# Five norms sum their squares over tiles on VectorE before the matmul with ones

## The chip, the cores and the metric

The kernel runs on one core of a Trainium2 chip, in one launch. The metric is the device time of an execution in microseconds (us), the median over several runs. The engines named here are TensorE (PE in the profile, PEld for its weight loads), VectorE (DVE), ScalarE (ACT), GpSimd (POOL) and SyncE (SP), which issues the transfers.

## The reference, cut to what matters

Two blocks are computed for 256 tokens of width 1024: a block with latent attention, a Fourier mixer and a hierarchical mixture of 32 experts, and then a two-layer block with a context of 256 tokens, attention, a convolution and several gated FFNs (width 2816). Between the parts stands the same norm, with a modulation by shift and scale:

```python
def rmsnorm_2(x, g):
    x32 = x.astype(jnp.float32)
    y = x32 * lax.rsqrt(jnp.mean(x32 * x32, axis=-1, keepdims=True) + EPS)
    return (y * g.astype(jnp.float32)).astype(x.dtype)

def modulate_2(x, g, shift, scale):
    return rmsnorm_2(x, g) * (1 + scale) + shift

def swiglu(x, w_gate, w_up, w_down):
    return (jax.nn.silu(x @ w_gate) * (x @ w_up)) @ w_down

def macaron_ffn(xs, g, shift, scale, gate, w_gate, w_up, w_down):
    return xs + 0.5 * gate * swiglu(modulate_2(xs, g, shift, scale), w_gate, w_up, w_down)
```

There are twelve norms in the kernel, numbered 0 to 11. The change is about norms 2 to 6: 2 is the context's ahead of its FFN, 3 the one that ends the first block, 4 the latent's ahead of its first FFN, 5 and 6 those of context and latent ahead of the attention.

## The kernel before

The state is held transposed: HT (latent) and CT (context) are SBUF tiles of 128 partitions by 8 tiles by 256 tokens, so that the 1024 features lie over partitions and tiles. Each engine has its program in a fixed, handwritten order, and works through it in that order; semaphores tie the engines together.

**Weights.** They come as pages of 128x2048 in float32 from device memory. SyncE issues a page into one of three slots of `raw`; ScalarE copies it rounded into `W` (`split`, L1494, or L1616 for the experts) and GpSimd subtracts that from the page for the remainder (`rest`, L632; L685 and, for the last expert unit in halves, L690 in the trace). TensorE takes each product three times: high by high, low by high, high by low (`mm3`, L703 to L705). A slot comes free when GpSimd has read it, and a place in W when TensorE has used it.

**A norm**, in the order of its steps:
- ScalarE squares the state into `XR`, two of the eight tiles at a time (`norm_squares`, L1466), each of the four steps with an increment of the semaphore `norm_squares` (`s_sq`).
- TensorE multiplies each of the eight tiles of XR with a 128x128 tile of ones and lets them add up in PSUM (`norm_chunk`, L737). This gives each partition the sum over all 1024 features. Float32 operands make two records of each of these matmuls in the trace, 16 for a norm.
- ScalarE takes the root (`norm_root`, L1476), for which it loads another activation table.
- VectorE makes the gains NA_ from scale and weight (`norm_head`, L1868), the reciprocal of the root (`norm_coef`, L1847), and scales the eight tiles (`norm_tiles`, L1879).
- ScalarE adds the shift with rounding (`norm_scaled`, L1485), VectorE makes the remainder (`norm_low`, L1858). Norm 3 has no remainder; its result is the state HT itself, and behind it ScalarE makes the squares of norm 4 at once.

**An FFN pass** (`ff_pass`: ctx_ff, ff00, ff01, ff10, ff11) has 11 units of three pages. In a unit TensorE makes the gate and up products of two halves (j = 0, 1) in PSUM banks, ScalarE the Silu of each (L1513) and behind it the split of the page three places on, VectorE multiplies, rounds and subtracts (L1925 to L1927, the last one makes HL), and TensorE makes the down products. Between them TensorE takes a column product of the modulation (`mod_product`, L728) whose vector VectorE summed in the unit before (`mod_sum`, L1826 and L1828) and takes from PSUM in this one (`mod_take`, L1837).

**Where the five norms stand.** Norms 3 and 4 stand in the pass ctx_ff, behind its units 0 and 2, and norm 5 in ff00, behind unit 1: on TensorE as `mid_norm`, which first waits for the unit's modulation and then makes the eight matmuls, on VectorE behind the unit's `mod_sum`, and on ScalarE behind the unit's last split and ahead of the next unit's Silu. Norm 2 stands among the last expert units: squares on ScalarE in unit 35, the matmuls on TensorE behind unit 37's first steps and the down products of unit 36, the root in unit 37. Norm 6 stands behind ff00: TensorE makes one product of the attention's projection (kac0), the norm, and another one (kac1).

Of the kernel before, what the change touches and what calls it, by code (L numbers as in the profile page):

```python
# [23 lines left out]
S = 256  # L24
# [72 lines left out]
NUNIT = GSLOTS * NE8  # L97
# [5 lines left out]
def build(nc, pages, mpages, acts, vecs, mbias, small):  # L103
# [4 lines left out]
    with ctx:  # L108
# [5 lines left out]
        def sem(name):  # L114
            if name not in sems:
                sems[name] = ctx.enter_context(nc.semaphore(name))
            return sems[name]
# [151 lines left out]
        def bias_of(h):  # L269
# [26 lines left out]
                                                  sem("group_aux"), sem("group_aux_copied"))  # L296
        s_silu = sem("silu_done")
        s_sq = sem("norm_squares")
        s_rt, s_ri, s_xr, s_yf, s_y = (sem("norm_root"), sem("norm_coef"), sem("norm_scaled"), sem("norm_result"),
                                         sem("norm_split"))  # L300
        s_xs = sem("norm_plain")
# [157 lines left out]
        def opened(pe, name, i=0):  # L459

            if prev_free[name, i] is not None:
                pe.wait_ge(*prev_free[name, i])
            return bank(name, i)
# [24 lines left out]
        NCH = 4  # L488
# [3 lines left out]

        SPLITS = [sum(1 for x in NORMS[:n] if x[1] in OPERANDS) for n in range(len(NORMS) + 1)]
        N_SMALL, N_MID = 10, 4
        MID_NORM = {"ctx_ff": ((1, "ss3"), (3, "ss4")), "ff00": ((2, "ss5"),), "ff01": (), "ff10": (), "ff11": ()}


# [200 lines left out]
        def _(pe):  # L698
# [40 lines left out]
                    last.then_inc(s_tile, 1)  # L739

            def norm(n):
                for c in range(NCH):
                    norm_chunk(n, c)

# [1047 lines left out]
        def _(dve):  # L1792
# [47 lines left out]
            def mod_step(m, vectors=(1,), i=0):  # L1840

                mod_sum(m, vectors, i)
                mod_take(m - 1, i, len(vectors))

            def norm_coef(n):
                dve.wait_ge(*tiles[f"ss{n}", 0][2])
                v.reciprocal(RT[:, 0:S], RT[:, 0:S]).then_inc(s_ri, 1)  # L1847
                dve.wait_ge(s_ri, n + 1)
# [40 lines left out]
            def residual(name, coef):  # L1889

                dst, col = coef
                for q in range(4):
                    ps = filled(dve, name, q)
                    for b in range(2):
                        k = 2 * q + b
                        last = v.scalar_tensor_tensor(out=dst[:, k, :], in0=ps[:, b * S:(b + 1) * S], scalar=col(k),
                                                      in1=dst[:, k, :], op0=ALU.mult, op1=ALU.add)
                    free(last, name, q)
# [4 lines left out]
            def half_gate(c, vi=0):  # L1903
                link(v.tensor_scalar(HG[:], MODT[:, c:c + KD, vi], 0.5, None, ALU.mult))
                return lambda k: HG[:, k:k + 1]

            def ff_pass(name, between=()):
                p0, u0, n, src, acc, parts = PASSES[name]
                steps = 2
                hx0 = hx[0]  # L1910

                def unit(u, i, vectors):
                    U = u0 + u
                    for j in range(2):
                        done = [hx0 + steps * (2 * u + j)]

                        def step(ins):

                            done[0] += 1
                            ins.then_inc(s_hx, 1)  # L1920
                            dve.wait_ge(s_hx, i * 4 * steps + done[0])

                        dve.wait_ge(s_silu, i * 4 + (2 * U + j + 1))
                        sil, hid = SIL[:, j, :], PS[GU[j]][:, S:2 * S]
                        step(v.tensor_tensor(hid, hid, sil, ALU.mult))  # L1925
                        step(v.tensor_copy(HH[:, j, :], hid))
                        v.tensor_tensor(HL[:, j, :], hid, HH[:, j, :].bitcast(f32), ALU.subtract).then_inc(s_hid, 1)  # L1927
                    if vectors:
                        mod_take(MOD_AT[name] + u - 1, i, len(vectors[1]))
                        if MOD_AT[name] + u < NMODP and not (u == n - 1 and name in TAIL):  # L1930
                            mod_sum(MOD_AT[name] + u, vectors[0], i)

                units(dve, parts, unit, between)
                hx[0] += steps * 2 * n
# [328 lines left out]
            def expert_low(u, part):  # L2263
                dve.wait_ge(s_mhi, 2 * u + part + 1)
                v.tensor_tensor(PAIRL[u % 2][:, part].rearrange("p k n -> p (k n)"), expert_raw(u, part),
                                PAIRH[u % 2][:, part, :].bitcast(f32), ALU.subtract).then_inc(low_done(u, part)[0], 1)
# [7 lines left out]
            for u in range(NUNIT):  # L2274
                j, e = u // NE8, u % NE8
                dve.wait_ge(s_gsil, u + 1)
                if u:
                    dve.wait_ge(s_gturn, u)
                if e == 0:
                    dve.wait_ge(s_auxd, 2 * (j + 1))  # L2280
                v.scalar_tensor_tensor(out=HID, in0=SIL[:, u % 2, :].rearrange("p (j n) -> p j n", j=2), scalar=CWS[:, j, e:e + 1],
                                       in1=PS[2 + u % 2][:, :].rearrange("p (j g n) -> p j g n", j=2, g=2)[:, :, 1, :],
                                       op0=ALU.mult, op1=ALU.mult).then_inc(s_ghid, 1)
                if u == 0:
                    mod_sum(20, (0,))
                if u in MOD_UNITS:
                    k = MOD_UNITS.index(u)
                    vectors = (0,) if k < MOE_ADA else (1, 2)
                    mod_sum(MOD_AT["moe"] + k, vectors)
                    mod_take(MOD_AT["moe"] + k - 1, 0, len(vectors))  # L2290
                if j and e == 0:
                    out_low(j - 1)
                if j and 1 <= e <= 4:
                    if e == 1 and j == 1:
                        dve.wait_ge(s_modev, (ADA + 48) // 2)
                    add_tokens(j - 1, e - 1)
                if j + 1 < GSLOTS:
                    if e == 4:
                        onehot(j + 1)
                    elif e in (5, 6):  # L2300
                        gathered_lo(j + 1, e - 5)
                    elif e == 7:
                        aux_copy(j + 1)
                if (u + 2, 1) in BY_VECTOR:
                    expert_low(u + 2, 1)
                if u == NUNIT - 3:
                    norm_head(2)
                if u == NUNIT - 2:
                    norm_tiles(2, range(0, 5), low=False)
                if u == NUNIT - 1:  # L2310
                    norm_tiles(2, range(5, KD), low=False)
                    for q in range(KD):
                        norm_low(2, q)
# [5 lines left out]
            residual("acc_ctx", (CT, half_gate(MOD0 + 16, 1)))  # L2319
            ff_pass("ff00", (lambda: None, lambda: norm(5)))  # L2320
            residual("acc_00", (HT, half_gate(MOD0 + 16, 0)))
            mod_take(MOD_AT["mixer"] - 1)
            norm(6)
            dve.wait_ge(sem("in_mid"), 16 * N_MID)
# [300 lines left out]
```

## Time and profile before

| | |
|---|---|
| median of 3 runs | 2045.34 us (2042.76 to 2045.85) |
| the profiled execution | 2042.77 us, of which the span from first to last instruction is 2041.0 |
| mean granted TensorE clock | 0.989 of full speed |
| TensorE busy | 1968.1 us (96%) |
| TensorE weight loads | 1768.6 us (87%) |
| VectorE busy | 1020.0 us (50%) |
| ScalarE busy | 824.4 us (40%) |
| GpSimd busy | 1329.9 us (65%) |

The span is what the profiler saw of one execution; 1.8 us of its time lie outside. Matmul records overlap, so a busy time near the span says that the engine's queue was hardly ever empty, not that each matmul ran at its best. An idle stretch of an engine carries the name of what released it. The norms in question lie at 662 (norm 2), 711 (norm 3), 750 (norm 4), 932 (norm 5) and 1100 us (norm 6) of the span.

### The profile page before, as it was taken

The page shows a single profiled execution, that of the slowest core. Times are in us where ns is not written, and L with a number is a line of the kernel's source. Part 1 is how long each engine was busy: PE and PEld are TensorE (multiplying, and loading weights), DVE is VectorE, ACT ScalarE, POOL GpSimd, SP SyncE. Part 2 cuts the span into 40 slices and gives each one's busy share as a digit, 9 for nine tenths or more (in the row PEclk, how much of TensorE's full clock was granted, in tenths as well). Part 3 has the DMA queues.
Part 4 walks back from the last instruction along what each step waited for, and adds up shares of the span by engine and source line. Part 5 has one row for each costly group of instructions (what it writes and reads, how often), then busy time and mean ns, then how long its engine had stood idle before and what let it go on. Part 6 is the DMA issues. An engine that isn't in the chain of part 4 may idle for free.

```text
span 2041.0 us, 34520 instructions
## 1 busy us (share of the span) xinstructions
PE 1968.1 (96%) x13902; PEld 1768.6 (87%) x13902; DVE 1020.0 (50%) x2154; ACT 824.4 (40%) x874; POOL 1329.9 (65%) x310
## 2 busy tenths in 40 slices
PE   6999889999999999999999999899999999999998
PEld 4879767667676799999999769799999999999998
DVE  6767474558565465455336334453335334654212
ACT  4343354444444553334434332443344333434332
POOL 5727157776768668777775412377777777777884
PEclk8999899999999999999999999999999999999999
DMA  8537198989898655666665402156665666655552
GB/s 354 214 124 289 67 374 349 376 345 368 355 375 336 230 224 210 244 239 225 241 241 205 153 33 104 60 215 242 247 239 204 233 233 244 229 221 192 185 185 83
DMA packets 67414, 473.92 MB, mean 232 GB/s; under 512 B 8064, under 2 KB 9184, under 8 KB 10208
## 3 DMA queue, kind: packets, MB, share of 16 engines
q1 hardware_dynamic: 65344, 466.82, 60.2%
q10 hardware_dynamic: 1952, 5.44, 0.7%
q8 instruction: 85, 1.39, 0.3%
q14 instruction: 33, 0.27, 0.0%
HBM read 471.18 MB, written 1.05 MB: 231 GB/s over the span
## 4 chain that ended last, share of the span: by engine, by line
PE 48%; issue 23%; POOL 19%; DMA 6%; DVE 1%; ACT 1%; SPq 0%; POOLq 0%; ACTq 0%; DVEq 0%
POOL W L632 15%; PE bank L703 11%; PE bank L705 11%; PE bank L704 11%; DMA raw<-in_pages 6%; PE bank L1197 4%; POOL YC L685 2%; PE bank L709 2%; PE bank L711 2%; PE bank L710 2%; PE bank L737 1%; ACT W L1616 1%; PE bank L728 1%; PE bank L748 1%; POOL W L685 1%
## 5 line engine op out<-in xcount | busy, mean ns | idle before, releaser
L632 POOL TENSOR_TENSOR W<-raw,W 128x2048 fp32r<-128x2048 f32 x220 | 1014.0, 4614 | 518.9 <-ACT W L1494 518.8
L703 PE MATMUL bank<-YH,W 128*128 128x256 f32 x1936 | 551.2, 285 | 1.1 <-POOL W L632 0.8
L705 PE MATMUL bank<-YH,W 128*128 128x256 f32 x1936 | 547.7, 283 | 0.0
L704 PE MATMUL bank<-YL,W 128*128 128x256 f32 x1936 | 547.6, 283 | 0.0
L1494 ACT ACTIVATE W<-raw 128x2048 fp32r<-128x2048 f32 x220 | 420.1, 1909 | 302.0 <-PE bank L705 275.6
L703 PEld LDWEIGHTS bank<-YH,W 128*128 128x128 f32 x1936 | 371.0, 192 | 3.9 <-POOL W L632 1.2
L704 PEld LDWEIGHTS bank<-YL,W 128*128 128x128 f32 x1936 | 371.3, 192 | 0.4 <-issue 0.2
L705 PEld LDWEIGHTS bank<-YH,W 128*128 128x128 f32 x1936 | 371.2, 192 | 0.0
L1828 DVE SCALAR_TENSOR_TENSOR bank<-mraw,CA,bank 128x256 f32<-128x256 f32 x696 | 329.1, 489 | 20.3
L1925 DVE TENSOR_TENSOR bank<-bank,SIL 128x256 f32<-128x256 f32 x110 | 47.6, 433 | 540.9 <-ACT SIL L1513 540.9
L703 PE MATMUL bank<-HH,W 128*128 128x256 f32 x880 | 249.7, 284 | 0.5 <-DVE HL L1927 0.4
L705 PE MATMUL bank<-HH,W 128*128 128x256 f32 x880 | 245.6, 279 | 0.0
L704 PE MATMUL bank<-HL,W 128*128 128x256 f32 x880 | 245.4, 279 | 0.0
L1616 ACT ACTIVATE W<-raw 128x2048 fp32r<-128x2048 f32 x77 | 147.5, 1916 | 147.5 <-DMA raw<-in_pages 147.5
L685 POOL TENSOR_TENSOR W<-raw,W 128x2048 fp32r<-128x2048 f32 x30 | 137.2, 4590 | 89.8 <-ACT W L1616 89.8
L685 POOL TENSOR_TENSOR YC<-raw,W 128x2048 fp32r<-128x2048 f32 x33 | 150.6, 4585 | 67.9 <-ACT W L1616 67.9
L1513 ACT ACTIVATE SIL<-bank 128x256 f32<-128x256 f32 x110 | 42.2, 384 | 359.1 <-PE bank L705 357.6
L703 PEld LDWEIGHTS bank<-HH,W 128*128 128x128 f32 x880 | 165.7, 188 | 0.7 <-issue 0.4
L704 PEld LDWEIGHTS bank<-HL,W 128*128 128x128 f32 x880 | 165.6, 188 | 0.0
L705 PEld LDWEIGHTS bank<-HH,W 128*128 128x128 f32 x880 | 165.4, 188 | 0.0
L709 PE MATMUL bank<-W,YH 128*128 128x512 f32 (+1 forms) x392 | 150.3, 383 | 9.0 <-POOL YC L685 6.6
L703 PE MATMUL bank<-YC,W 128*128 128x256 f32 (+1 forms) x536 | 153.5, 286 | 1.0 <-DVE R L2015 1.0
(353 smaller groups left out, 3159.5 us busy)
## 6 DMA issues: line engine op xcount, KB each, us to landing
raw<-in_pages SPq DMA_DIRECT2D x299, 1024.0 KB, 4.9
mraw<-in_mpages SPq DMA_DIRECT2D x98, 1024.0 KB, 6.9
R<-in_pages SPq DMA_DIRECT2D x24, 1024.0 KB, 5.8
XR<-in_pages SPq DMA_DIRECT2D x17, 1024.0 KB, 5.5
R<-in_mpages SPq DMA_DIRECT2D x4, 1024.0 KB, 16.3
HT<-in_acts ACTq DMA_DIRECT2D x1, 1024.0 KB, 14.1
CT<-in_mpages SPq DMA_DIRECT2D x1, 1024.0 KB, 19.4
raw<-in_mpages SPq DMA_DIRECT2D x1, 1024.0 KB, 25.1
```

What stands on the lines that cost most here:

```text
L632: nc.gpsimd.tensor_tensor(WL[:, p % SLOTS, :], raw[:, p % SLOTS, :], WH[:, p % SLOTS, :].bitcast(f32), ALU.subtract).then_inc(s_lo, 1)
L685: p_.tensor_tensor(PAIRL[u % 2][:, part].rearrange("p k n -> p (k n)"), expert_raw(u, part), PAIRH[u % 2][:, part, :].bitcast(f32), ALU.su ...
L703: mm(out, w[0], x[0], start=start, stop=False, skip_group_check=True)
L704: mm(out, w[0], x[1], start=False, stop=False, skip_group_check=True)
L705: return mm(out, w[1], x[0], start=False, stop=stop, skip_group_check=True)
L709: mm(out, x[0], w[0], start=start, stop=False, skip_group_check=True)
L1197: last = mm(PS[OUT[n]][:, :], HTT[:, j, :], w[:, j * D + n * 512:j * D + n * 512 + 512], start=(u % NE8 == 0 and j == 0), stop=(u % NE8 == ...
L1494: f(WH[:, p % SLOTS, :], raw[:, p % SLOTS, :], ACT.Copy).then_inc(s_hi, 1)
L1513: f(SIL[:, j, :], PS[GU[j]][:, 0:S], ACT.Silu).then_inc(s_silu, 1)
L1616: f(PAIRH[u % 2][:, part, :], expert_raw(u, part), ACT.Copy).then_inc(s_mhi, 1)
L1828: last = v.scalar_tensor_tensor(out=out, in0=w[:, k, :], scalar=c, in1=part, op0=ALU.mult, op1=ALU.add)
L1925: step(v.tensor_tensor(hid, hid, sil, ALU.mult))
```

## The change

For norms 2 to 6 VectorE adds the eight tiles of squares to one, in place, in three linked steps: tiles 4 to 7 to tiles 0 to 3 (128x1024), then 2 and 3 to 0 and 1 (128x512), then 1 to 0 (128x256). A new semaphore tells TensorE, which then makes one matmul with ones in place of eight. `link` makes VectorE wait for the end of the instruction before it goes on. The steps stand behind the products HL and ahead of `mod_take` in unit 0 of ctx_ff (norm 3), unit 2 of ctx_ff (norm 4) and unit 0 of ff00 (norm 5); at the end of expert unit 36 (norm 2, NUNIT is 40); and straight behind the residual of ff00 (norm 6).

```diff
+        PRESUMMED = (2, 3, 4, 5, 6)
+        PRESUM_AT = {("ctx_ff", 0): 3, ("ctx_ff", 2): 4, ("ff00", 0): 5}
...
             def norm(n):
+                if n in PRESUMMED:
+                    ps = opened(pe, f"ss{n}")
+                    pe.wait_ge(s_presum, PRESUMMED.index(n) + 1)
+                    mm(ps[:, 0:S], ONES[:], XR[:, 0, :], start=True, stop=True, skip_group_check=True).then_inc(s_tile, 1)
+                    return
                 for c in range(NCH):
                     norm_chunk(n, c)
...
+            def presum(n):
+                dve.wait_ge(s_sq, NCH * (n + 1))
+                link(v.tensor_tensor(XR[:, 0:4, :], XR[:, 0:4, :], XR[:, 4:8, :], ALU.add))
+                link(v.tensor_tensor(XR[:, 0:2, :], XR[:, 0:2, :], XR[:, 2:4, :], ALU.add))
+                v.tensor_tensor(XR[:, 0, :], XR[:, 0, :], XR[:, 1, :], ALU.add).then_inc(s_presum, 1)
...
                         v.tensor_tensor(HL[:, j, :], hid, HH[:, j, :].bitcast(f32), ALU.subtract).then_inc(s_hid, 1)
+                    if (name, u) in PRESUM_AT:
+                        presum(PRESUM_AT[name, u])
                     if vectors:
                         mod_take(MOD_AT[name] + u - 1, i, len(vectors[1]))
...
                 if (u + 2, 1) in BY_VECTOR:
                     expert_low(u + 2, 1)
+                if u == NUNIT - 4:
+                    presum(2)
                 if u == NUNIT - 3:
                     norm_head(2)
...
             residual("acc_00", (HT, half_gate(MOD0 + 16, 0)))
+            presum(6)
             mod_take(MOD_AT["mixer"] - 1)
             norm(6)
```

The order of VectorE's instructions around norm 3, before the change (unit 0 of ctx_ff; HL is the second remainder of the unit, MODT the modulation taken, MACC its next sum, NA_ the gains, RT the root):

```order
L1927 TENSOR_TENSOR HL<-bank,HH 128x256
L1837 TENSOR_TENSOR MODT<-bank,MB 128x4
L1826 TENSOR_SCALAR bank<-mraw,CA 128x256
L1828 SCALAR_TENSOR_TENSOR bank<-mraw,CA,bank 128x256 x6
L1828 SCALAR_TENSOR_TENSOR MACC<-mraw,CA,bank 128x256
L1868 SCALAR_TENSOR_TENSOR NA_<-MODT,V 128x8
L1847 RECIPROCAL RT<-RT 128x256
```

and with the change (its line numbers are higher, as lines were added):

```order
L1941 TENSOR_TENSOR HL<-bank,HH 128x256
L1855 TENSOR_TENSOR XR<-XR 128x1024
L1856 TENSOR_TENSOR XR<-XR 128x512
L1857 TENSOR_TENSOR XR<-XR 128x256
L1845 TENSOR_TENSOR MODT<-bank,MB 128x4
L1834 TENSOR_SCALAR bank<-mraw,CA 128x256
L1836 SCALAR_TENSOR_TENSOR bank<-mraw,CA,bank 128x256 x6
L1836 SCALAR_TENSOR_TENSOR MACC<-mraw,CA,bank 128x256
L1882 SCALAR_TENSOR_TENSOR NA_<-MODT,V 128x8
L1861 RECIPROCAL RT<-RT 128x256
```

The three adds stand ahead of everything that leads to the reciprocal. The order of TensorE's instructions at the same place before, from the last down product of unit 0 (HH, HL) to the first gate product of unit 1 (YC):

```order
L704 MATMUL bank<-HL,W 128x256
L705 MATMUL bank<-HH,W 128x256
L737 MATMUL bank<-XR,ONES 128x256 x8
L703 MATMUL bank<-YC,W 128x256
L704 MATMUL bank<-YC,W 128x256
```

and with the change:

```order
L707 MATMUL bank<-HL,W 128x256
L708 MATMUL bank<-HH,W 128x256
L748 MATMUL bank<-XR,ONES 128x256
L706 MATMUL bank<-YC,W 128x256
L707 MATMUL bank<-YC,W 128x256
```

Eight matmuls became one, and nothing else moved. VectorE's instructions at norm 6 with the change, behind the residual of ff00 (before, the three adds are missing and the rest is the same):

```order
L1910 SCALAR_TENSOR_TENSOR HT<-bank,HG,HT 128x256 x8
L1855 TENSOR_TENSOR XR<-XR 128x1024
L1856 TENSOR_TENSOR XR<-XR 128x512
L1857 TENSOR_TENSOR XR<-XR 128x256
L1845 TENSOR_TENSOR MODT<-bank,MB 128x2
L1882 SCALAR_TENSOR_TENSOR NA_<-MODT,V 128x8
L1861 RECIPROCAL RT<-RT 128x256
```

Here too the take of the modulation, the gains and the reciprocal stand behind the adds.

## Rows read from the trace of the kernel before

**Rows 1.** TensorE timeline, norm 2: start, duration (us), engine, line, operation, tiles.

```profile
662.28 3.62 PE L737 MATMUL bank<-XR,ONES 128*128 128x256 f32 x16
...
665.54 0.58 PE L709 MATMUL bank<-W,YH 128*128 128x512 f32 x1
```

**Rows 2.** TensorE timeline, norm 3; in brackets: idle time ahead, its releaser.

```profile
710.72 3.62 PE L737 MATMUL bank<-XR,ONES 128*128 128x256 f32 x16
...
726.55 0.36 PE L703 MATMUL bank<-HH,W 128*128 128x256 f32 x1 [0.37 <-DVE HL L1927]
```

**Rows 3.** Timeline of ScalarE (ACT) at norm 3.

```profile
714.37 0.47 ACT L1476 ACTIVATE RT<-bank,EPSC 128x256 f32<-128x256 f32 x1 [0.24 <-PE bank L737]
...
724.64 0.38 ACT L1513 ACTIVATE SIL<-bank 128x256 f32<-128x256 f32 x1
```

**Rows 4.** Timeline of VectorE (DVE) at norm 3.

```profile
705.76 0.42 DVE L1927 TENSOR_TENSOR HL<-bank,HH 128x256 fp32r<-128x256 f32 x1
...
710.23 2.23 DVE L1868 SCALAR_TENSOR_TENSOR NA_<-MODT,V 128x8 f32<-128x8 f32 x1
714.95 1.75 DVE L1847 RECIPROCAL RT<-RT 128x256 f32<-128x256 f32 x1 [2.49 <-ACT RT L1476]
```

**Rows 5.** Source view (ns min/median/max), GpSimd's (POOL) timeline, VectorE's groups by form.

```profile
L2058 DVE TENSOR_TENSOR XR<-XR,ST x6: 691/692/2573, 108.5 to 129.7; 128x512 f32<-128x512 f32 x6
...
105.99 4.51 POOL L632 TENSOR_TENSOR W<-raw,W 128x2048 fp32r<-128x2048 f32 x1 [1.61 <-ACT W L1494]
...
L1887 DVE TENSOR_TENSOR YL<-XR,YH 128x1024 fp32r<-128x1024 f32 x1 | 1.2, 1224 | 0.0
```

**Rows 6.** Timeline of VectorE and of GpSimd in expert work.

```profile
301.02 4.50 DVE L2192 TENSOR_SCALAR R<-CT,R 128x128 f32<-128x128 f32 x1
305.44 4.61 DVE L2192 TENSOR_SCALAR R<-CT,R 128x128 f32<-128x128 f32 x1
305.39 4.57 POOL L685 TENSOR_TENSOR W<-raw,W 128x2048 fp32r<-128x2048 f32 x1
```

**Rows 7.** Window view (busy by engine, then granted clock); TensorE's timeline there.

```profile
300.00:310.00 10.00, 7.64 (x21) 4.59 (x20) 9.96 (x4) 3.83 (x2) 10.00 (x4) 0.83 0.86 340
...
305.53 0.47 PE L709 MATMUL bank<-W,YH 128*128 128x512 f32 x1 [2.36 <-POOL YC L685]
```

**Rows 8.** Timeline of GpSimd at norm 3.

```profile
703.28 9.15 POOL L632 TENSOR_TENSOR W<-raw,W 128x2048 fp32r<-128x2048 f32 x2 [3.58 <-ACT W L1494]
...
712.90 4.58 POOL L632 TENSOR_TENSOR W<-raw,W 128x2048 fp32r<-128x2048 f32 x1 [0.47 <-ACT W L1494]
```

**Rows 9.** Timeline of GpSimd at norm 2.

```profile
652.87 9.15 POOL L685 TENSOR_TENSOR W<-raw,W 128x2048 fp32r<-128x2048 f32 x2
661.96 2.37 POOL L690 TENSOR_TENSOR YH<-raw,W 128x1024 fp32r<-128x1024 f32 x1
```

**Rows 10.** Timeline of VectorE and of GpSimd at norm 4.

```profile
745.29 0.42 DVE L1927 TENSOR_TENSOR HL<-bank,HH 128x256 fp32r<-128x256 f32 x1
754.48 1.75 DVE L1847 RECIPROCAL RT<-RT 128x256 f32<-128x256 f32 x1 [3.58 <-ACT RT L1476]
746.28 4.59 POOL L632 TENSOR_TENSOR W<-raw,W 128x2048 fp32r<-128x2048 f32 x1 [1.02 <-ACT W L1494]
```

**Rows 11.** Timeline of VectorE, GpSimd and TensorE at norm 5.

```profile
909.75 0.42 DVE L1927 TENSOR_TENSOR HL<-bank,HH 128x256 fp32r<-128x256 f32 x1
916.45 4.62 POOL L632 TENSOR_TENSOR W<-raw,W 128x2048 fp32r<-128x2048 f32 x1 [1.17 <-ACT W L1494]
926.14 0.36 PE L703 MATMUL bank<-HH,W 128*128 128x256 f32 x1
```

**Rows 12.** Timeline of GpSimd and TensorE at norm 6.

```profile
1095.74 4.63 POOL L632 TENSOR_TENSOR W<-raw,W 128x2048 fp32r<-128x2048 f32 x1 [1.17 <-ACT W L1494]
1099.95 3.61 PE L737 MATMUL bank<-XR,ONES 128*128 128x256 f32 x16
...
1111.65 0.39 PE L703 MATMUL bank<-YH,W 128*128 128x256 f32 x1 [0.17 <-DVE YL L1858]
```

More of the change, by code:

```diff
@@ L298, in build @@
         s_sq = sem("norm_squares")
+        s_presum = sem("squares_summed_over_tiles")
         s_rt, s_ri, s_xr, s_yf, s_y = (sem("norm_root"), sem("norm_coef"), sem("norm_scaled"), sem("norm_result"),
```

## The prediction

> **What bounds the kernel now.** I read the page's totals first, then each engine's timeline around the five norms, because a share of busy time doesn't say which wait ends last at one place. TensorE is the busiest engine, and a norm with eight matmuls holds it for a clear stretch: norm 2's first record starts at 662.28 us and the next work at 665.54, so 3.26 us [rows 1]. One of the eight is an eighth of that, about 0.41 us. If TensorE's queue alone sets the pace, the removal is therefore worth 3.26 - 0.41 = 2.85 us of TensorE at each norm, 14.3 us for five.
>
> At norm 3 it doesn't. The norm's matmuls run at 710.72, and TensorE then has a unit's gate and up products to do, which don't need the norm. But at 726.55 it stood idle for 0.37 us, waiting for HL of VectorE [rows 2]. That HL hangs on another chain, which begins with the norm: ScalarE takes the root at 714.37 (0.24 us behind the last norm matmul; its activation table had only just been loaded), VectorE takes the reciprocal at 714.95, eight tiles are scaled and the next norm's squares made, and only then does ScalarE, in its program order, get to the unit's Silu at 724.64 [rows 3, 4]. So behind a norm inside an FFN pass two chains of nearly the same length meet. Shortening TensorE's alone turns the gain into a wait; what counts is when VectorE can take the reciprocal. The reader should keep that in mind: any delay of VectorE before 714.95 moves 726.55 one for one.
>
> **What the adds cost VectorE.** Alone, an add of 128x1024 should take the 1.22 us of a VectorE subtraction of that shape, and one of 128x512 the 0.69 us of the median in the same group [rows 5]; for 128x256 I take 0.42 us, the time of the subtraction HL [rows 4]. Sum 2.33 us, some 2.4 with the waits between. But the adds read two SBUF tiles, and the trace shows what such a VectorE instruction does while GpSimd works. The six multiplications of 128x512 take 0.691 us, except the first, 2.573: it was issued at 108.5 while GpSimd was in a subtraction from 105.99 to 110.50, and it ended about 0.6 us after that one [rows 5]. Two small ones that came one behind the other took 4.50 and 4.61 us [rows 6]. The first had been waiting since 301.02 and was done at 305.52, though GpSimd had issued its next page at 305.39; the second was issued at 305.44, 0.05 us behind that page, and waited until the page's end at 309.96. So: such an instruction waits until the running GpSimd instruction ends, whoever was issued first goes first, and between two of them a waiting GpSimd instruction gets in. Three linked adds then pay the rest of one GpSimd instruction and up to two whole ones of 4.57 us.
>
> The Trainium skill (SBUF — State Buffer, Who interferes with whom) speaks against this change in the same way: a VectorE instruction with two SBUF inputs contends with a GpSimd instruction that reads SBUF, and the pair of ports is held for the whole instruction. By this rule the three adds would take 6 to 13 us where GpSimd's queue is full, and 2.4 us without it. The trace agrees, with 2.573 us against 0.691.
>
> **TensorE's clock.** A wait of TensorE of 2.36 us at 305.53 lies in a stretch of 10 us with a mean granted clock of 0.83: 1.7 us of work lost, as a part of it ran at 1.2 instead of 2.4 GHz [rows 7]. I charge 1.7 us once for each new wait over 2 us, less what slack there is behind it.
>
> **Norm 3 (first unit of ctx_ff).** Everything of the adds stands before the take of the modulation, its sum, the gains NA_ and the reciprocal. The last HL ends at 706.18 [rows 4]. GpSimd has two pages from 703.28 to 712.43, the second from about 707.85, and a third is ready at 712.90 [rows 8]. First add: waits until 707.85, ends 709.07. GpSimd's second page moves to 709.07-713.64. Second add ends 714.33, third page ends 718.9, third add ends 719.3. TensorE can't start its norm matmul at 710.72 but at about 719.5. On VectorE the take and the sum need 4.1 us (706.1 to 710.23) [rows 4]; they now end at 723.5, NA_ at 723.7, as GpSimd is then idle. The reciprocal moves from 714.95 to 723.8, by 8.85 us. Before, the first scaled tile also waited about 0.55 us for the third page (ending 717.48); this wait is gone. So Silu and the unit's down products move by **+8.3 us**. TensorE's own work (0.4 + 11.7 us from 719.5, with the slow clock 1.7 more) ends near 733.3 and is hidden by that.
>
> **Norm 2 (expert unit 36).** The adds are issued while GpSimd is in the first of two pages (652.87 to 662.02, the second from about 657.45); then come four half pages of 2.4 us, the first at 661.96 [rows 9]. First add 657.45-658.67, page to 663.24, second add to 663.93, a half to 666.3, third add to 666.72. The norm's matmul starts at 666.8 and not 662.28; the next work at 667.25 against 665.54: +1.7, and +1.7 for the clock, as no chain runs in parallel here. **+3.4 us.** GpSimd's last half ends near 674, before it is needed: the products that want it stood behind two more steps of TensorE.
>
> **Norm 4 (third unit of ctx_ff).** HL ends at 745.71, just when GpSimd has a gap until 746.28 [rows 10]. First add to 746.9, the page moved to 751.45, second add to 752.14, third, before the next page is ready, to 752.6. TensorE waits until 752.8, but its own saving pays for that. The sum then ends at 756.8, NA_ waits for the next page, and the reciprocal comes at 757.4 instead of 754.48: 2.9 late, less the 0.55 as above. **+2.3 us.** If the next page got in before the third add (they are some 0.3 us apart), it would be about 4.6 us more.
>
> **Norm 5 (first unit of ff00).** HL ends at 910.17. The page then in work holds the second add until about 916.7; the next page was ready at 916.45, gets in, and the third add ends at 921.6 [rows 11]. The modulation sum stands behind it until 925.8, and the next unit's HL, in the same queue, is ready at 927.3; TensorE wanted it at 926.14. **+0.9 us**, since the root's chain behind the norm takes back what TensorE saves.
>
> **Norm 6 (behind ff00).** The squares are done while GpSimd is in a page until 1100.37 [rows 12]; the first add waits for that, then GpSimd is idle, the three end at 1102.8, and one matmul at 1103.2, where the eight from 1099.95 also released TensorE's next work (3.26 us later). Nothing won. The wait of 2.8 us costs 1.7 in clock, less some 0.7 of slack at the wait for YL at 1111.65 [rows 12]. **+1.0 us.**
>
> **Sum.** 3.4 + 8.3 + 2.3 + 0.9 + 1.0 = +15.9 us. The profiled execution took 2042.8 (span 2041.0) and would take 2058.7; against the median of 2045.34 the forecast is 2061. Bounds of this case: without any clock loss norm 2 is +1.7 and norm 6 nothing, and with norm 5 at -0.2 the sum is +12.1; with norm 4's page getting in (+4.6) and the clock's loss doubled at norm 2 (+1.7) it is +22.2. Its own range is 2056 to 2068.
>
> **Rivals.**
> - *The adds don't wait (or hardly).* For it: five of the six multiplications of 128x512 took 0.69 us. Against it: the sixth, and both small ones [rows 5, 6]. Then norm 2 gives -2.85; norms 3, 4 and 5 only the 0.24 of the root or nothing, as the chain binds; norm 6 up to -1.5, because its matmul would be early. Together -5: 2040. Chance 0.10.
> - *All of TensorE's saving counts*: the same, and the norm's chain is shorter than I read it. -14: 2031. Chance 0.04. It needs the 0.37 us wait for HL to be an accident [rows 2].
> - *Only part of the waits come*: GpSimd doesn't get in between linked adds, so each norm pays one wait. Norm 3's adds end at 710.2; the sum, and then the third page, which moves behind them to 714.8-719.4, put the first scaled tile at 719.4 instead of 717.48: +1.9. Norm 2's end at 659.8: -2.85. Norm 4 +0.5, norm 5 -0.2, norm 6 +1.0 as above: +0.4, 2046. Chance 0.12. It is right if the next add is taken before a page that already waits; against it speaks the second small one [rows 6].
> - *Forecast*: chance 0.74.
>
> About 0.2% (4 us) can be told from no change here. Slower by more than that: 0.74 and nearly half of the partial case, 0.79. Faster: the second rival and over half of the first, 0.10. Within: 0.11. The forecast's range with the partial case added holds 8 in 10: 2045 to 2069.
>
> **What would show it.** In the trace of after: adds with 4 to 6 us each beside 1.2, 0.7 and 0.4; TensorE idle for about 9 us ahead of norm 3's matmul, 4.5 at norm 2, 2.5 at norms 4 and 6, hardly at 5; the reciprocal of norm 3 some 9 us after where it was; the granted clock below 1 behind norms 2, 3 and 6. I am wrong if the adds take 2.4 us in sum, or if the page at norm 3 isn't in GpSimd's queue when the add is.

## The result, and the profile with the change

The changed kernel took **2058.02 us** in the median of five runs (2055.72 to 2065.63), the kernel before on the same chip 2042.76 us (2038.91 to 2045.85, five runs). The ratio is 1.0085, with a 95% interval of 1.0066 to 1.0105: slower, by 0.85%. The ratio is that of the means, 2060.07 and 2042.75 us, which are 17.3 us apart; the medians are 15.3 us apart. The forecast was 2061, +15.9 us by its sum.

The profiled execution took 2055.72 us, with this span and these totals on the profile's first page:

```profile
span 2053.9 us, 34395 instructions
...
PE 1962.9 (96%) x13832; PEld 1762.8 (86%) x13832; DVE 1045.0 (51%) x2169; ACT 824.7 (40%) x874; POOL 1333.7 (65%) x310
```

TensorE's busy time fell by only 5.2 us, although five times 2.85 us of matmuls are gone: it ran part of the rest at the lower clock (mean granted clock 0.983, before 0.989). VectorE's rose by 25 us for fifteen instructions that need 11.7 us by themselves.

The source view of VectorE's three adds (duration in ns, least, median and longest, then the first and last start):

```profile
L1855 DVE TENSOR_TENSOR XR<-XR x5: 1216/2866/4961, 650.7 to 1111.4; 128x1024 f32<-128x1024 f32 x5
...
L1856 DVE TENSOR_TENSOR XR<-XR x5: 691/4926/4991, 655.7 to 1114.3; 128x512 f32<-128x512 f32 x5
...
L1857 DVE TENSOR_TENSOR XR<-XR x5: 424/424/4599, 660.7 to 1115.1; 128x256 f32<-128x256 f32 x5
```

The shortest of each are the 1.22, 0.69 and 0.42 us of the forecast, to the hundredth. The longest are those with a wait for GpSimd in them. Norm 3 has the worst of it. The timelines of VectorE, GpSimd, TensorE and ScalarE there, which answer to [rows 2, 3, 4, 8]:

```profile
705.16 0.42 DVE L1941 TENSOR_TENSOR HL<-bank,HH 128x256 fp32r<-128x256 f32 x1
705.51 2.87 DVE L1855 TENSOR_TENSOR XR<-XR 128x1024 f32<-128x1024 f32 x1
708.41 4.93 DVE L1856 TENSOR_TENSOR XR<-XR 128x512 f32<-128x512 f32 x1
713.37 4.60 DVE L1857 TENSOR_TENSOR XR<-XR 128x256 f32<-128x256 f32 x1
...
722.21 1.75 DVE L1861 RECIPROCAL RT<-RT 128x256 f32<-128x256 f32 x1
...
702.68 15.00 POOL L635 TENSOR_TENSOR W<-raw,W 128x2048 fp32r<-128x2048 f32 x3 [3.57 <-ACT W L1502]
...
718.11 1.20 PE L748 MATMUL bank<-XR,ONES 128*128 128x256 f32 x2 [7.83 <-DVE MODT L1845]
...
719.35 0.48 ACT L1484 ACTIVATE RT<-bank,EPSC 128x256 f32<-128x256 f32 x1 [5.82 <-PE bank L748]
...
731.36 0.39 ACT L1521 ACTIVATE SIL<-bank 128x256 f32<-128x256 f32 x1
```

The two engines take turns. Three pages lie in 15.00 us without an idle time between them (before, two of them in 9.15, then a gap and the third), and the three adds, in place of 2.33 us, take 12.40 in the same stretch. Counted from HL, which before stood at 705.76 and now at 705.16, the reciprocal is 7.86 us later than in [rows 4] (722.21 - 705.16 = 17.05, before 9.19), and the Silu 7.32 us later than in [rows 3].

The waits of TensorE between 650 and 1200 us (total, times, longest); of these, before had only one for HL, the 0.37 us of [rows 2]:

```profile
PE bank L748 <- DVE MODT L1845: 9.9, 2, 7.8
PE bank L748 <- DVE XR L1857: 6.4, 2, 3.7
PE bank L706 <- DVE HL L1941: 6.0, 2, 3.1
```

The first two lines are the waits for the adds: 7.8 at norm 3 and 2.0 at norm 4 (MODT stands behind the third add and is named in its place), 3.7 at norm 2 and 2.7 at norm 6. The third line is what the forecast didn't have. The rows of it in TensorE's timeline, behind norms 4 and 5, and the window view behind the second (stretch, its length, busy time, granted clock, DMA share, GB/s):

```profile
774.63 0.36 PE L706 MATMUL bank<-HH,W 128*128 128x256 f32 x1 [2.94 <-DVE HL L1941]
...
957.73 0.58 PE L706 MATMUL bank<-HH,W 128*128 128x256 f32 x1 [3.09 <-DVE HL L1941]
...
955.00:960.00 5.00, 2.27 (x10) 0.63 0.15 61
960.00:964.00 4.00, 4.00 (x25) 0.61 0.11 16
964.00:967.00 3.00, 3.00 (x28) 1.00 0.82 328
```

**Where the time came from.** HL is made in each unit, behind the unit's whole work, so its starts serve as milestones. I counted them from the last addition to the state HT ahead of norm 2 (652.85 before, 649.94 with the change), since nothing is changed ahead of it, and the start of that addition alone varied between 649.9 and 655.4 us over the ten profiles of this study. VectorE's timeline before, and then with the change: that addition, and HL in the first two units behind norm 4:

```profile
652.85 0.87 DVE L2239 SCALAR_TENSOR_TENSOR HT<-bank,MODT,HT 128x256 f32<-128x256 f32 x2 [3.48 <-PE bank L1117]
...
765.24 0.42 DVE L1927 TENSOR_TENSOR HL<-bank,HH 128x256 fp32r<-128x256 f32 x1
...
778.79 0.42 DVE L1927 TENSOR_TENSOR HL<-bank,HH 128x256 fp32r<-128x256 f32 x1
```

```profile
649.94 0.88 DVE L2255 SCALAR_TENSOR_TENSOR HT<-bank,MODT,HT 128x256 f32<-128x256 f32 x2 [3.48 <-PE bank L1125]
...
774.06 0.42 DVE L1941 TENSOR_TENSOR HL<-bank,HH 128x256 fp32r<-128x256 f32 x1
...
789.16 0.42 DVE L1941 TENSOR_TENSOR HL<-bank,HH 128x256 fp32r<-128x256 f32 x1
```

The first is 8.82 us later, and 8.82 + 2.91 (the earlier start) = 11.73; the second 10.37 + 2.91 = 13.28. The same reckoning over the whole stretch:

| milestone | shift, us | step |
|---|---|---|
| unit 0 of ctx_ff (behind norm 2) | +2.31 | norm 2: 2.3 |
| unit 1 (behind norm 3) | +9.62 | norm 3: 7.3 |
| unit 3, first half (behind norm 4) | +11.73 | norm 4: 2.1 |
| unit 4 | +13.28 | clock behind norm 4: 1.55 |
| unit 2 of ff00 (behind norm 5) | +13.33 | norm 5: 0.05 |
| unit 3 | +15.75 | clock behind norm 5: 2.4 |
| behind norm 6 | +16.26 | norm 6: 0.5 |

So the stretch costs 16.3 us. The span grew by 12.9, as this execution reached the stretch 2.9 us earlier and lost 0.45 us less behind the stretch; the medians differ by 15.3.

### The profile page after: what moved, and what is told of

It reads as the page before. It is cut to its first block, busy times and chain, and to the rows that moved or that the text cites. A ratio compares the mean times of both kernels' runs of the same rounds, so it can differ in the third digit from the quotient of the medians.

```text
span 2053.9 us, 34395 instructions
## 1 busy us (share of the span) xinstructions
PE 1962.9 (96%) x13832; PEld 1762.8 (86%) x13832; DVE 1045.0 (51%) x2169; ACT 824.7 (40%) x874; POOL 1333.7 (65%) x310
## 4 chain that ended last, share of the span: by engine, by line
PE 46%; issue 24%; POOL 19%; DMA 7%; DVE 2%; ACT 1%; SPq 0%; POOLq 0%; ACTq 0%; DVEq 0%
POOL W L635 15%; PE bank L706 11%; PE bank L708 11%; PE bank L707 11%; DMA raw<-in_pages 6%; PE bank L1205 3%; POOL YC L688 2%; PE bank L712 2%; PE bank L714 1%; PE bank L713 1%; POOL W L688 1%; ACT W L1624 1%; PE bank L731 1%; PE bank L740 1%; PE bank L756 1%
```

## The experiments

Eight kernels follow. They are compared by the milestones above, each read from one profiled execution, and, where several executions were timed, by the ratio of the means to runs of the kernel before on the same chip.

### Does a reduction that doesn't wait for GpSimd save the change?

```diff
-                    mm(ps[:, 0:S], ONES[:], XR[:, 0, :], start=True, stop=True, skip_group_check=True).then_inc(s_tile, 1)
+                    mm(ps[:, 0:S], ONES[:], RT[:, S:2 * S], start=True, stop=True, skip_group_check=True).then_inc(s_tile, 1)
...
-                link(v.tensor_tensor(XR[:, 0:4, :], XR[:, 0:4, :], XR[:, 4:8, :], ALU.add))
-                link(v.tensor_tensor(XR[:, 0:2, :], XR[:, 0:2, :], XR[:, 2:4, :], ALU.add))
-                v.tensor_tensor(XR[:, 0, :], XR[:, 0, :], XR[:, 1, :], ALU.add).then_inc(s_presum, 1)
+                v.tensor_reduce(RT[:, S:2 * S], XR[:].rearrange("p k t -> p t k"), AX.X, ALU.add).then_inc(s_presum, 1)
```

> The change with one VectorE tensor_reduce over the eight tiles (one SBUF input, result in the free half of RT) in place of the three adds; same five places, same sum, one matmul. Port theory (the adds cost what they cost because they read two SBUF tiles while GpSimd works): the reduce takes its own 2.2 to 2.8 us everywhere, TensorE doesn't wait for it at norms 2, 3 and 4, and the change's +15 us is gone but for the waits for HL behind norms 3, 4 and 5 (2.5 to 3 us each, with a fall of the granted clock behind them): -3 to +3 us against the kernel before. Rival (the mere length of VectorE's extra work ahead of the modulation counts): within 4 us of the changed kernel, so some 15 us slower than before.

Measured: 2050.22 us (median of ten; before 2041.48 of 25), ratio 1.0041 [1.0023, 1.0060]. The source view of the reduction, VectorE's and GpSimd's timelines and TensorE's next wait at norm 3:

```profile
L1855 DVE TENSOR_REDUCE RT<-XR x5: 3718/3918/3935, 653.0 to 1106.9; 128x256 f32<-128x2048 f32 x5
...
710.39 3.50 DVE L1880 SCALAR_TENSOR_TENSOR NA_<-MODT,V 128x8 f32<-128x8 f32 x1
...
709.24 4.63 POOL L635 TENSOR_TENSOR W<-raw,W 128x2048 fp32r<-128x2048 f32 x1 [0.43 <-ACT W L1502]
...
724.98 0.55 PE L706 MATMUL bank<-HH,W 128*128 128x256 f32 x1 [5.49 <-DVE HL L1939]
```

The first half of the theory holds: five times the same 3.7 to 3.9 us, though a page of GpSimd ran for all or part of each. The reduction by itself is longer than the 2.2 to 2.8 us that I had expected, and longer than the 2.33 us of three free adds. The Trainium skill (SBUF — State Buffer, Who interferes with whom) says that a reduction never contends on this chip; the trace agrees, with these five. The waits for GpSimd thus cost the change nearly 8 of its 16 us (its stretch is at +16.3, this one at +8.6).

The second half, that the rest would be about nothing, fell. Norm 2 gained 3.0 us, norm 6 0.5. Norms 3 and 4 cost 2.1 us each: the take and the sum of the modulation stand 3.8 us later, and NA_, with two SBUF operands, is issued 1.15 us behind a page (norm 3, above; 754.44 against 753.29 at norm 4) and is held until that page's end, 3.50 and 3.48 us. And behind each of norms 3, 4 and 5 TensorE waited for HL, by 5.49, 5.21 and 3.08 us, and 2.4, 2.7 and 2.7 us more were lost behind these waits, where the granted clock was 0.50 to 0.52 over the next 4 us. This kernel has the TensorE saving almost whole, and it is slower.

### Is it the removed matmuls that cost behind norms 4 and 5?

Made of the changed kernel: the one matmul is made eight times over the same tile at norms 4 and 5, each time anew.

```diff
-                    mm(ps[:, 0:S], ONES[:], XR[:, 0, :], start=True, stop=True, skip_group_check=True).then_inc(s_tile, 1)
+                    for _ in range(KD if n in (4, 5) else 1):
+                        last = mm(ps[:, 0:S], ONES[:], XR[:, 0, :], start=True, stop=True, skip_group_check=True)
+                    last.then_inc(s_tile, 1)
```

> The change, but at norms 4 and 5 TensorE makes the one matmul eight times over into the same place (result unchanged), so that it is as busy there as before. Theory that the time TensorE saved at these norms became a wait for HL of about 3 us, and the wait a fall of the granted clock: no wait above 0.5 us for HL behind norms 4 and 5, no stretch at half clock there, and 3 to 4 us faster than the changed kernel, though it does 14 matmuls more. Rival (matmuls cost time, the clock falls for other reasons): as the change or up to 5.7 us slower.

Measured: 2052.21 us (median of ten), ratio 1.0053 [1.0035, 1.0072]. TensorE's waits for HL, and the window behind norm 4, first of this kernel, then of the changed one:

```profile
PE bank L706 <- DVE HL L1943: 1.2, 1, 1.2
...
750.00:800.00 50.00, 47.97 (x393) 1.00 0.60 229
```

```profile
750.00:800.00 50.00, 45.03 (x366) 0.97 0.58 224
```

The one wait for HL that is left, 1.17 us at 733.90, stands behind norm 3, where the two kernels are alike; behind norms 4 and 5 there is none. The milestones go to +11.95 behind norm 4 and stay there (+11.98 behind norm 5 and to the last unit), where the change goes from +11.73 to +13.28 and +15.75. With fourteen matmuls more, the 4.0 us behind these two norms are gone: this loss is the clock's, and the removal of the matmuls brought it.

At norm 6, where the code of the two kernels is the same too, they differ all the same: the change loses 0.5 us there, this one gains 0.1. TensorE's wait for the adds is of one length, 2.68 and 2.69 us. The windows behind it, first of the changed kernel, then of this one:

```profile
1116.00:1120.00 4.00, 4.00 (x23) 0.59 1.01 422
```

```profile
1112.00:1116.00 4.00, 3.81 (x30) 1.00 1.00 422
```

So a wait of this length was followed by the lower clock in one execution and not in the other, and a difference of 0.6 us between two profiles can come from that alone.

### The removal alone

Made of the kernel before, without any add: norms 3, 4 and 5 multiply only the first tile of squares.

```diff
+        ONE_TILE = (3, 4, 5)
...
             def norm(n):
+                if n in ONE_TILE:
+                    ps = opened(pe, f"ss{n}")
+                    pe.wait_ge(s_sq, NCH * (n + 1))
+                    mm(ps[:, 0:S], ONES[:], XR[:, 0, :], start=True, stop=True, skip_group_check=True).then_inc(s_tile, 1)
+                    return
```

> The kernel before, without any adds, but norms 3, 4 and 5 multiply only the first of the eight tiles of squares with ones (seven tiles are left out of these sums, so the output differs). It shows the removal alone. Theory (the chain root, reciprocal, scaling, Silu, HL ends last there): the three norms' 8.5 us of TensorE come back as waits for HL of 2.5 to 3 us each, and with the clock's fall it is 0 to 5 us slower than before. Rival (TensorE is the bound): 8 us faster.

Measured: 2046.59 us (median of ten), ratio 1.0027 [1.0009, 1.0046]: slower, with three times 2.85 us less work on the busiest engine. TensorE's waits for HL, and two windows behind the first of them, which ends at 726.70:

```profile
PE bank L704 <- DVE HL L1933: 9.7, 3, 3.4
...
728.00:731.50 3.50, 3.50 (x23) 0.67 0.00 0
731.50:735.00 3.50, 3.50 (x32) 1.00 0.70 206
```

At each norm the milestone right behind it moved by 0.03 to 0.05 us, and the one after that by 1.56, 1.54 and 1.53 more. The whole removed work came back as a wait of 3.1 to 3.4 us, and that wait was followed by a stretch at the lower clock, in which 23 matmuls take the time of 32. Three times 1.6 us are the 4.8 us that the stretch lost.

### Norm 3 by itself, and the cause of its waits

Three kernels have the change at norm 3 alone (`PRESUMMED = (3,)`): as it stands; with the second operand of each add taken from PSUM (which leaves out the sum of squares: what is added isn't the other tiles); and with the adds behind the modulation's take and sum.

```diff
+                other = PS[MISC][:, 0:S].unsqueeze(1)
-                link(v.tensor_tensor(XR[:, 0:4, :], XR[:, 0:4, :], XR[:, 4:8, :], ALU.add))
+                link(v.tensor_tensor(XR[:, 0:4, :], XR[:, 0:4, :], other.broadcast_to([P, 4, S]), ALU.add))
...
```

```diff
-                    if (name, u) in PRESUM_AT:
-                        presum(PRESUM_AT[name, u])
                     if vectors:
                         mod_take(MOD_AT[name] + u - 1, i, len(vectors[1]))
...
+                    if (name, u) in PRESUM_AT:
+                        presum(PRESUM_AT[name, u])
```

As it stands:

> The change at norm 3 alone. Port theory: HL of ctx_ff's second unit comes 7.3 us later than before (measured from HL of the first unit), as in the changed kernel, and no other stretch is longer: +7 to +9 us on the span. Rival (the five places act on each other): another figure, below +5 or above +11.

Operand from PSUM:

> The change at norm 3 alone, with the three additions of the same shapes in the same place, but their second operand comes from a PSUM bank (old partial sums of the modulation), so that each reads one SBUF tile. The sum of squares is left out by that, so norm 3's result is wrong. Port theory: the three take 1.2, 0.7 and 0.4 us in spite of GpSimd, HL of ctx_ff's second unit comes 0.2 us earlier to 0.3 later than before, TensorE waits some 3 us for it, and the clock's fall costs about 1.5 us: +1.5 us in all. Rival (length and place of the additions, whatever they read): +7.4 us at that HL, as with the change at norm 3 alone.

Adds behind the modulation's sum:

> The change at norm 3 alone, with the three additions behind the modulation's take and sum (ahead of the gains) and not ahead of them. Port theory, worked out from the trace of before: VectorE comes to them at 710.2, GpSimd's second page ends at 712.4, first add to 713.6, third page to 718.2, second add to 718.9, third to 719.4 with GpSimd idle, norm matmul and root to 720.8, reciprocal then in place of 722.8: HL of the second unit +5.3 us where the change has +7.4. Rival (the additions' waits are a fixed cost wherever they stand): +7.4.

Measured, one profiled execution each. As it stands: the stretch +7.42 us (+7.36 behind norm 3, and flat from there on); the execution took 2056.54 us, but it was 1.9 us late ahead of the stretch and lost 4.4 us behind it, where nothing is changed, so that single time doesn't size the effect. The cost of norm 3 is thus its own and adds up with the others.

With the operand from PSUM: VectorE's and GpSimd's timelines and TensorE's wait behind the norm:

```profile
705.64 1.21 DVE L1856 TENSOR_TENSOR XR<-XR,bank 128x1024 f32<-128x1024 f32 x1
706.88 0.69 DVE L1857 TENSOR_TENSOR XR<-XR,bank 128x512 f32<-128x512 f32 x1
707.61 0.42 DVE L1858 TENSOR_TENSOR XR<-XR,bank 128x256 f32<-128x256 f32 x1
...
702.83 9.20 POOL L635 TENSOR_TENSOR W<-raw,W 128x2048 fp32r<-128x2048 f32 x2 [3.60 <-ACT W L1502]
...
726.15 0.36 PE L706 MATMUL bank<-HH,W 128*128 128x256 f32 x1 [3.45 <-DVE HL L1943]
```

GpSimd is in its pages from 702.83 to 712.03, and the adds pass beside them in 2.4 us. So for these adds it is the second SBUF operand that makes them wait, not their shape, their place, or VectorE's turn on something else. This isn't shown for every kind of instruction: in the kernel before, one with a single SBUF tile waited too (below, at the ports). The milestone behind the norm moves by 0.05 us, and the clock behind the 3.45 us wait adds 1.57: +1.67 in the stretch.

With the adds later, VectorE's timeline and TensorE's norm matmul:

```profile
712.79 3.27 DVE L1855 TENSOR_TENSOR XR<-XR 128x1024 f32<-128x1024 f32 x1
716.09 4.87 DVE L1856 TENSOR_TENSOR XR<-XR 128x512 f32<-128x512 f32 x1
720.99 0.42 DVE L1857 TENSOR_TENSOR XR<-XR 128x256 f32<-128x256 f32 x1
...
721.56 1.19 PE L748 MATMUL bank<-XR,ONES 128*128 128x256 f32 x2 [8.12 <-DVE XR L1857]
```

The first HL behind the norm came at +5.34, as worked out, but the second at +7.10, and the stretch ended at +7.44 like the plain version. TensorE had waited 8.12 us for the adds and came back at the lower clock (0.50 from 720 to 724 us), and the second Silu then waited 1.64 us for its gate and up products. That part of the expectation missed: two chains of nearly one length, and I had moved only one.

### A version meant to beat the kernel before

By the results so far the change can only pay where no chain runs beside TensorE (norm 2) and with a reduction that doesn't wait. First norms 2 and 6, then norm 2 alone (`PRESUMMED = (2,)`), both with the reduction and the matmul of the first experiment. The edit for the first, cut to its first lines:

```diff
-        PRESUMMED = (2, 3, 4, 5, 6)
-        PRESUM_AT = {("ctx_ff", 0): 3, ("ctx_ff", 2): 4, ("ff00", 0): 5}
+        PRESUMMED = (2, 6)
+        PRESUM_AT = {}
...
```

> Sum by tensor_reduce and one matmul at norms 2 and 6 only; norms 3, 4 and 5 as in the kernel before. Theory (only where TensorE's queue ends last is a matmul worth its time, and the reduce doesn't touch GpSimd's port): 3.0 us won at norm 2, about 0.5 at norm 6, nothing else moves: -3.5 us, 0.17%, against the kernel before, no fall of the clock behind the norms. Rival (the reduce's 3.9 us on VectorE delays something there): 0 or slower.

> The kernel before with one tensor_reduce in place of the eight tiles at norm 2 alone (norm 6 is as before). In the version with norms 2 and 6 the trace showed -3.12 us at norm 2 and +0.14 at norm 6, but the times did not show it: ratio 1.0004 [0.9989, 1.0018]. Theory: the 3.1 us are real and norm 6 adds nothing, so the trace again shows -3.1 us from norm 2 on, flat to the end of the stretch, and the times come out at -3 us, ratio 0.9985, with an interval of some 0.15% on either side. Rival: something outside of the stretch that no view of it shows gives the gain back; then the trace still shows -3.1 in the stretch, but the ratio is 1.000 or above in this timing too.

Measured: norms 2 and 6 took 2042.20 us (median of 12; before 2042.25 of 17), ratio 1.0004 [0.9989, 1.0018]; norm 2 alone 2039.51 us (12; before 2042.56 of 17), ratio 0.9986 [0.9972, 1.0001]. In the trace norm 2 gives -3.12 and -2.93 us, flat to the end of the stretch; norm 6 takes 0.14 back. TensorE's timeline at norm 2 of the second kernel, and at norm 6 of the first:

```profile
656.77 3.60 PE L1205 MATMUL bank<-R,WRT 128*128 128x512 f32 x8
660.21 0.59 PE L748 MATMUL bank<-RT,ONES 128*128 128x256 f32 x2
```

```profile
1096.68 0.67 PE L748 MATMUL bank<-RT,ONES 128*128 128x256 f32 x2 [2.31 <-DVE RT L1855]
```

At norm 2 the reduction is over by 655.4 and the matmul follows the work ahead of it without a wait; its removed time is a gain from end to end. At norm 6 TensorE waits 2.31 us and its clock falls (0.55 from 1097.5 to 1101 us), so the 0.5 us expected there didn't come. In the first experiment the same code at norm 6 had the same wait of 2.31 us, the clock stayed at 1.00 from 1110 to 1120 us, and the 0.5 us was won. The three microseconds that the trace shows are the 0.14% that the second timing has as its middle; its interval ends at 1.0001, and the first timing's middle was 1.0004. Single runs of one kernel differ by up to 13 us here. So the gain is shown in the trace, and the times agree with it for norm 2 alone without proving it: that this version beats the kernel before in time is not shown.

## Why the prediction was right, and where its sizes were off

**The ports.** Right in kind for the adds and nearly in size. The adds waited for GpSimd at every norm: all three at norms 2 and 3, the second at 4 and 5, the first at 6; and GpSimd got in between linked adds. The turns were slightly shorter than I had them: I charged a whole page of 4.57 us plus the add's own time (5.26 and 4.99 us for the second and the third), and the rows show 4.91 to 4.99 and 4.60. Norm 3's adds thus took 12.4 us from the end of HL instead of 13.1, and the norm cost 7.3 instead of 8.3.

One piece of the evidence was misread. I called the small instructions of [rows 6] examples of reading two SBUF tiles. They are comparisons of one tile with a column of scalars. And L2190, just above them in the kernel, takes one 128x2 tile and constants alone. It ran four times, for 0.78 to 4.20 us, and ended each time within 0.1 us of the end of a GpSimd page; the longest, and its page, which ended at 397.78 (timelines of VectorE and GpSimd, kernel before):

```profile
393.61 4.20 DVE L2190 TENSOR_SCALAR R<-R 128x2 f32<-128x2 f32 x1
393.14 4.64 POOL L685 TENSOR_TENSOR W<-raw,W 128x2048 fp32r<-128x2048 f32 x1 [0.79 <-ACT W L1616]
```

So a second SBUF tile isn't needed for such a wait. For the adds the conclusion stood on the multiplications of [rows 5], which do read two, and the experiment with the operand in PSUM bears it out.

**Norm 2.** +3.4 forecast, +2.3 measured: the later start 1.3 instead of 1.7 us, the clock 1.0 instead of 1.7. TensorE's timeline there, which answers to [rows 1]:

```profile
663.27 1.19 PE L748 MATMUL bank<-XR,ONES 128*128 128x256 f32 x2 [3.71 <-DVE XR L1857]
663.90 0.99 PE L712 MATMUL bank<-W,YH 128*128 128x512 f32 x1
```

The next work starts 13.96 us behind the addition to the state (663.90 - 649.94), before 12.69, so 1.3 later; the rest of the 2.3 comes behind it, where the granted clock was 0.81 from 665 to 668 us. Both terms were right in kind; the charge of 1.7 us for the clock, from one wait elsewhere [rows 7], was a rough price for a wait of 3.71 us.

**Norms 4 and 5: the step that failed.** The forecast had +2.3 and +0.9, with the sentence, at norm 5, that "the root's chain behind the norm takes back what TensorE saves". That is right (+2.1 and +0.05 at the milestone behind each), but I priced this taking back at nothing. At norm 5 TensorE's saving becomes a wait for HL of 3.09 us. At norm 4 2.0 us of it go into the wait for the adds, but the chain is 2.1 us later, so TensorE waits 2.94 us for HL there. By my own rule of a charge for each new wait over 2 us both had to be charged as well. They cost 1.55 and 2.4 us. With eight matmuls in place of one the charge vanished, and with the removal alone it came three times.

**Norm 5's adds.** I let the page in ahead of the third add; VectorE won by 0.08 us. The timelines of VectorE and GpSimd of the changed kernel:

```profile
921.71 4.99 DVE L1856 TENSOR_TENSOR XR<-XR 128x512 f32<-128x512 f32 x1
926.74 0.42 DVE L1857 TENSOR_TENSOR XR<-XR 128x256 f32<-128x256 f32 x1
...
921.04 5.11 POOL L635 TENSOR_TENSOR W<-raw,W 128x2048 fp32r<-128x2048 f32 x1 [1.15 <-ACT W L1502]
...
926.82 4.84 POOL L635 TENSOR_TENSOR W<-raw,W 128x2048 fp32r<-128x2048 f32 x1 [0.67 <-ACT W L1502]
```

The page comes where it did before, 6.70 us behind HL (926.82 - 920.12, before 916.45 - 909.75 [rows 11]). The second add ends 6.58 us behind HL where I had 6.95, by the same shorter turn, so the third is issued ahead of the page and now the page waits (4.84 us instead of 4.6). The 1.15 us by which the next unit's HL was to be late came out at 0.2, gone within the unit.

**Norm 6.** +1.0 forecast, +0.5 measured, with the wait at 2.68 us where I had 2.8; but this size was partly luck: with the same code and the same wait the kernel with the fill gained 0.1 us, as its clock didn't fall.

**The sum.** 15.9 forecast and 16.3 measured in the stretch, in part by luck: the terms that I had were 3.6 us too high together (1.1, 1.0, 0.2, 0.8 and 0.5 for norms 2 to 6), and the 4.0 us of clock behind norms 4 and 5 weren't in it. Of the rivals, "the adds don't wait" falls by the rows above; its own figure of -5 was wrong too, since norm 3 with adds that pass in 2.4 us still cost 1.67 us and not nothing. "All of TensorE's saving counts" is refuted most plainly by the removal alone. "Only one wait per norm" is what came at norms 4, 5 and 6, but norms 2 and 3 paid for each add.

## What to carry to other kernels

Where an engine is 96% busy but another chain ends at nearly the same time, work removed from it comes back as a wait, and on TensorE the wait itself had a price: here each removal of 2.85 us at such a place made the kernel 1.5 to 2.7 us slower behind the wait, at the lower clock. So ask at each place which wait would end last with the work gone, and price the new wait too, not only those ahead of the changed instruction. Before handing work to VectorE beside a busy GpSimd, count the SBUF operands: the linked adds with two of them paid up to a whole GpSimd instruction each, while the reduction, and the adds with one operand in PSUM, paid none. One SBUF operand is no guarantee by itself, since the `tensor_scalar` of L2190 with a single tile waited; look for the instruction's own rows beside GpSimd.

## What the runs showed of the hardware that was not expected

- A reduction of eight tiles in one instruction (128x256 from 128x2048, float32) takes 3.72 to 3.94 us with GpSimd at work beside it for all or part of that time; three adds of the same tiles take 2.33 us free and 12.4 us at norm 3 beside it.
- The turn between VectorE and GpSimd goes by issue, to less than a tenth of a microsecond: the add issued 0.08 us ahead of a page passed in 0.42 us, and the one issued while a page ran took 4.9.
- The waits run both ways: pages that took 4.6 us took 5.00, 5.11 and 4.84 us where an add stood ahead of them.
- A VectorE instruction with one SBUF tile of 128x2 elements and constants waited until a GpSimd page ended (up to 4.20 us).
- Removing 2.85 us of TensorE's work at a place where its clock was full made the kernel slower by 1.5 us, three times in one kernel, by the lower clock behind the wait.
- Waits of one length were followed by different losses: behind norm 5 a wait of 3.08 us cost 1.53 us with the removal alone, and one of 3.08 us cost 2.72 with the reduction.
- Behind all nine waits for HL of 2.9 us or more the clock was lower. Behind the waits at norm 6 it was lower in two executions (2.68 and 2.31 us) and full in two others with waits of the same two lengths (2.69 and 2.31 us). What decides stays open; no run here varied it.
